# Second attention, last eight steps: score products of two steps in one group, in four banks instead of two

## What is computed

```python
s_sel = jnp.einsum('bgrqd,bgqkd->bgrqk', qb, k_sel) * scale
p_sel = masked_softmax(s_sel, (kpos <= qpos[:, None])[:, :, None])
o_sel = jnp.einsum('bgrqk,bgqkd->bgrqd', p_sel.astype(dt), v_sel)
...
p_win = masked_softmax(s_win, wmask)
o_win = jnp.einsum('bgrqk,bgkd->bgrqd', p_win.astype(dt), v_win)
...
o = g[0] * o_cmp + g[1] * o_sel + g[2] * o_win
```

## Time and profile before

| what | us |
|---|---|
| median of 3 runs (1046.75 to 1049.96) | 1046.78 |
| the profiled execution | 1047.31 |
| its span in the profile | 1045.5 |
| TensorE busy | 1034.8 (99%) |
| VectorE busy | 641.1 (61%) |
| ScalarE busy | 522.2 (50%) |
| GpSimd busy | 346.7 (33%) |

### The profile page before, as it was taken

The page is one execution under the profiler, slowest core; times in us unless marked ns, Lnnn a source line. Parts: engine busy times, 40 slices in busy tenths (PEclk is TensorE's granted clock), DMA queues, the critical chain, the costliest instruction groups (busy, mean ns, idle before and its releaser), DMA issues. The chain is left out here.

```text
span 1045.5 us, 14416 instructions
## 1 busy us (share of the span) xinstructions
PE 1034.8 (99%) x5362; PEld 849.0 (81%) x5362; DVE 641.1 (61%) x1129; ACT 522.2 (50%) x945; POOL 346.7 (33%) x334
## 2 busy tenths in 40 slices
PE   9999999999999999999999999999999999999997
PEld 7788888888878898988787788888888888888885
DVE  5578998666765233514567888344322325999976
ACT  7454345455662333434567874224443446554554
POOL 0022110004330003700264520008779945753542
PEclk9999999999999999999999999999999999999999
DMA  9654322223320384133200461249999942443542
GB/s 331 117 113 118 101 81 71 71 59 124 133 91 1 109 262 141 41 81 81 61 1 2 125 223 55 81 132 326 352 355 339 329 139 61 151 135 137 201 181 82
DMA packets 99639, 146.26 MB, mean 140 GB/s; under 512 B 6209, under 2 KB 60225, under 8 KB 99569
## 3 DMA queue, kind: packets, MB, share of 16 engines
q1 hardware_dynamic: 86016, 129.70, 38.2%
q10 hardware_dynamic: 12768, 12.88, 3.9%
q0 software_dynamic: 784, 2.75, 1.7%
HBM read 123.69 MB, written 21.63 MB: 139 GB/s over the span
## 5 line engine op out<-in xcount | busy, mean ns | idle before, releaser
L2371 DVE TENSOR_TENSOR w_lo<-wring,w_hi 128x1024 fp32r<-128x1024 f32 x32 | 49.0, 1530 | 112.4 <-ACT w_hi L1780 112.4
L1926 DVE TENSOR_TENSOR u_lo<-wring,u_hi 128x1024 fp32r<-128x1024 f32 (+1 forms) x64 | 79.4, 1249 | 53.1 <-ACT u_hi L1505 52.5
L853 PE MATMUL bank<-u_hi,h_hi 128*128 128x512 f32 (+1 forms) x288 | 110.9, 385 | 0.1
L853 PE MATMUL bank<-u_hi,h_lo 128*128 128x512 f32 (+1 forms) x288 | 109.1, 379 | 0.0
L853 PE MATMUL bank<-u_lo,h_hi 128*128 128x512 f32 (+1 forms) x288 | 109.0, 378 | 0.0
L1505 ACT ACTIVATE u_hi<-wring 128x1024 fp32r<-128x1024 f32 (+1 forms) x64 | 65.8, 1032 | 82.7 <-PE bank L853 70.6
L853 PE MATMUL bank<-h_hi,w_lo 128*128 128x512 f32 (+2 forms) x272 | 104.5, 384 | 0.0
L853 PE MATMUL bank<-h_hi,w_hi 128*128 128x512 f32 (+2 forms) x272 | 104.4, 384 | 0.0
L853 PE MATMUL bank<-h_lo,w_hi 128*128 128x512 f32 (+2 forms) x272 | 104.3, 384 | 0.0
L853 PE MATMUL bank<-h_hi,u_hi 128*128 128x512 f32 x224 | 94.1, 420 | 0.3 <-ACT arena L1447 0.2
L1339 PE MATMUL bank<-s_hi,f_hi 128*128 128x512 f32 x224 | 88.5, 395 | 0.1
(11 more groups left out here) (351 smaller groups left out, 2459.4 us busy)
## 6 DMA issues: line engine op xcount, KB each, us to landing
wring<-in_w_in SPq DMA_DIRECT2D x60, 512.0 KB, 3.9
wring<-in_w_ff ACTq DMA_DIRECT2D x12, 1024.0 KB, 8.4
wring<-sums_kept SPq DMA_DIRECT2D x16, 768.0 KB, 4.2
wring<-in_w_ff SPq DMA_DIRECT2D x22, 512.0 KB, 6.1
wring<-in_w_ff SPq DMA_DIRECT2D x32, 256.0 KB, 3.3
sums_kept<-wring SPq DMA_DIRECT2D x22, 256.0 KB, 5.6
arena<-in_w_out SPq DMA_DIRECT2D x4, 1024.0 KB, 5.1
wring<-in_w_out SPq DMA_DIRECT2D x2, 2048.0 KB, 13.0
```

The costliest lines, as they stand in the source:

```text
L853: last = mm(b, lhs, rhs, start=(start and n == 0), stop=(stop and n == 2))
L1926: v.tensor_tensor(u_lo[u % RAW_UNITS][:, 0:cols], raw_unit(u), u_hi[u % HI_UNITS][:, 0:cols].bitcast(F32), ALU.subtract).then_inc(u_lo_don ...
L2371: v.tensor_tensor(cut(w_lo[ring3(m)]), src, cut(w_hi[ring3(m)]).bitcast(F32), ALU.subtract).then_inc(w_lo_done, 1)
```

## The change

In the last eight steps (t from 56, NS - NH), the score products of t = 56 and 58 go out together at t = 56, and those of 60 and 62 at t = 60. The second pair of each group (steps 58, 59, 62, 63) goes to banks 0 and 1, those of the filling products, so TensorE waits for `a_free` at A2_END at t = 56 and t = 60. The waits for `l_done` at t = 58 and 62 fall away. Every pair still raises `s_full` by 2 at its end.

```diff
             i = steps2[u][0]
             at = 256 if i <= 1 and u % 4 >= 2 else 0
-            return bank[2 + u % 2][:, at:at + (i + 1) * P]
+            b = u % 2 if u >= NS - NH and u % 4 >= 2 else 2 + u % 2
+            return bank[b][:, at:at + (i + 1) * P]
...
                 if t < NS:
                     grouped = steps2[t][0] <= 1
-                    if not grouped or t % 4 == 0:
+                    if t % 4 == 0 or not grouped and t < NS - NH:
                         pe.wait_ge(l_done, NS + t)
-                    if not grouped:
+                    if t >= NS - NH and t % 4 == 0:
+                        pe.wait_ge(a_free, A2_END)
+                        pair2(t, 2)
+                        pair2(t + 2, 2)
+                    elif not grouped and t < NS - NH:
                         pair2(t, 2)
                     elif t % 4 == 0:
                         pair2(t, 0)
```

## The result

| | us |
|---|---|
| before, median of 10 (1046.6 to 1049.96) | 1046.96 |
| after, median of 10 (1049.3 to 1052.0) | 1051.01 |
| ratio after to before | 1.0033, 95% interval 1.0024 to 1.0043 |
| profiled execution of after, and its span | 1049.33, 1047.5 |

The kernel became slower: by the ratio 0.33%, 3.5 us (2.5 to 4.5), and by the two medians 4.05 us. The forecast was +2.6. The ten executions of after don't scatter about one value: three lie at 1049.3, the other seven between 1050.5 and 1052.0, and the mean TensorE clock of six of these is 0.997 where that of the three is 0.999. The profiled execution is one of the three, so its trace shows the loss without what the other seven add.

The account below looks back on a forecast made before the run. TensorE, busy 99% of the span, was taken to bound the kernel, with VectorE and ScalarE nearly full in the changed stretch. 2.50 (wait) + 0.13 (legs) = +2.6 us on 1046.78 gave 1049.4 us, range 1047.7 to 1050.9.

Parts of the forecast that it names:

- The new wait: At t = 56 TensorE waits for ScalarE to take the last filling product: pair 56 starts 2.50 us late.
- The lag from the take to TensorE: Before pair 56: TensorE starts 0.65 us after ScalarE's copy of the last filling product starts.
- The legs: Pair 56 to pair 60, 6.37 us against 6.49; pair 60 to branch product, 8.25 against 8.00; together +0.13.
- The order that binds: VectorE's in-order queue sets the first leg, up to pair 60; ScalarE's copies set the second, up to the branch product.
- second leg: From pair 60 to the first branch product: 8.25 us after the change against 8.00 before.
- The change of row mode: Between 64-row and 128-row products, 0.10 us each; falls out inside a group, saving 0.20 us of TensorE's work a group.
- No absorption later: After the branch product: a delay of the attention's last steps reaches the kernel's end in full.
- Rival A: Pair 56 to branch product: TensorE alone binds, late start paid back to +0.9 us, 1047.7; chance 0.15.
- Rival B: Both groups: second pair lies on the chain, nothing given back, +4.1 us, 1050.9; chance 0.15.
- Rival D: At t = 56 the wait costs nothing, only grouping's +0.2 us is left, 1047.0; chance 0.05.
- Rival C: At the stop before pair 56 the clock falls to 1.2 GHz: +2.5, together +5.1 us, 1051.9; chance 0.05.

Follow-up runs that it names:

- the early take: Changed kernel with the last chunk of the last filling product at t = 52 instead of 54, so ScalarE takes it earlier: 1046.88 us, ratio 1.0002.
- e1: The changed kernel again, unaltered, low clock in its trace: five executions from 1050.43 to 1051.19 us, ratio 1.0037 to before.
- e11: The changed kernel once more, unaltered, low clock in its trace: one execution at 1049.36 us, four from 1051.04 to 1051.82, ratio 1.0039 to before.
- the early chunk alone: Kernel before with the last chunk of the last filling product at t = 52 instead of 54, no grouping: 1046.64 us, ratio 0.9999.
- the early-take kernel with the late collect: The early take plus VectorE's collect and GpSimd's addition moved behind scores 58 and 59: 1046.3 us, ratio 0.9993 to before.
- the late collect alone: Kernel before with VectorE's collect and GpSimd's addition moved behind scores 58 and 59, no grouping: ratio 1.0002 to before.

## Why the prediction was right, and where it was not

**The new wait** is what it said, at its place and by its releaser: 2.50 us late forecast, 2.59 measured (pair 52 to pair 56 is 9.56 us against 6.97). The lag from the take to TensorE is 0.74 us (592.06 to 592.80), not 0.65: the one row I took it from the earlier trace rows was 0.1 short for this pair.

**The legs.** Forecast 6.37 and 8.25, measured 6.43 and 8.37: +0.31 against before instead of +0.13. The order that binds is the one named, VectorE's at pair 60 and ScalarE's after; the group at 60 alone shows the second leg's 8.37 again. The change of row mode fell out inside the group, as said.

**No absorption later.** From the branch product to the end of the span: 440.2 us before, 439.9 after. The 2.90 us of the stretch appear in full; that the span grew by only 2.0 is because this run was at pair 52 0.60 us earlier and 0.3 shorter at the end, and traces of other kernels differ by as much.

**Rival A** (TensorE alone binds, +0.9) didn't happen in the changed kernel: it waits 0.51 and 0.45 us again behind the stop. Half of its mechanism is real: with the wait alone, TensorE gains 0.62 us back. **Rival B** (+4.1, both second pairs on the chain) didn't happen either, 14.80 us instead of 16; but 0.93 of its 1.58 us is what grouping costs against the wait alone. **Rival D** is the early take: +0.28 against +0.2 forecast.

**Rival C, the clock, is the step that failed.** I gave it 0.05, and by their times it comes in 16 of 20 executions (two of them traced). The argument was: at the kernel's end the clock fell about four microseconds after the last product, and the stop is 2.5, so it will hold. In the two traces here the clock fell 3.9 us (e1) and 2.3 us (e11) after TensorE had stopped, in e1 when it was at work again. And the one row that the argument rests on is one of a wide spread: in the fourteen traces of this case the clock at the kernel's end falls between 2.2 and 5.2 us after the last product. The shortest is the early chunk alone (last product over at 1038.96), the longest the early-take kernel with the late collect (1038.44). Their windows in which the clock falls, columns as above:

```profile
1041.00:1042.00 1.00, 0.00 (x0) 0.00 (x0) 0.74 (x1) 0.71 (x1) 0.00 (x0) 0.56 0.80 301
```

```profile
1043.00:1044.00 1.00, 0.00 (x0) 0.00 (x0) 0.00 (x0) 0.00 (x0) 0.00 (x0) 0.83 0.53 197
```

Two of the fourteen are shorter than the stop of 2.52 us, so "shorter than four" was no cover. The Trainium skill, page "TensorE: Matmul & The Clock Gate", section "Why this matters for your kernels", warns of stops between bursts, but of longer ones than this; here 2.52 us was enough, and the measurement decides.

C's price was too high for the two traced executions. A low stretch of 3.4 us costs 0.86 and 1.39 us there, not 2.5: it is shorter than the 5 us taken from the kernel's start, and part of it falls on time in which TensorE waits anyway (the wait at pair 60 is 0.27 us in e1 instead of 0.51). The windows at the kernel's start read a granted clock of 1.00, so the earlier trace rows doesn't show what a low clock costs.

**What was luck.** By the ratio the forecast was 0.9 us short, and the time, 1046.78 x 1.0033 = 1050.2, lies in the range. The median of after itself, 1051.01, lies 0.1 above its upper end. That end is rival B's price, and B didn't happen; what brings the time there is C, which the range left out. "Within 0.3%" had 0.73, and 0.33% with an interval from 0.24 to 0.43 doesn't decide it. So the mechanism of the wait and of the legs was right, the traced execution without a low clock (1049.33) is the forecast's 1049.4, and a good part of the upper group's distance from it was not foreseen.

## What to carry to other kernels

A wait that is "already met" where it stands may not be so a few instructions earlier: look up when the releasing engine's queue reaches the release, not when the data were ready. Here the data of (gb, 7) were in PSUM over three microseconds before ScalarE, with exponentials ahead in its queue, took them out. Giving a producer a second pair of banks cost 0.61 us here with the collect ahead in the consumer's queue, and was worth nothing (0.03 us) with it out of the way. And a stop of a few microseconds on TensorE, otherwise 99% busy, must be priced with its clock: behind a stop of 2.52 us it cost another 0.86 and 1.39 us in the two traces, in some executions and not in others. A median then lies in the larger group and hides the other.

## What was not expected of the hardware

After a stop of 2.52 us with TensorE busy on both sides, 14 of 20 executions have a mean clock of 0.997 and 16 are high; in the two of them that were traced the clock is at 0.50 of full speed for 3.4 us, once beginning before work resumed and once 1.4 us after it. None of nine executions with the same stop filled by ten matmuls is high, and none of nine with 1.26 us of stop is at 0.997; one of each was traced. The time from the last product of the kernel to the fall behind it isn't fixed either: 2.2 to 5.2 us in fourteen traces. Single high executions occur in kernels without a stop too (1049.96 and 1049.79 of before, 1049.41 of the late collect alone, 1048.67 of the early take), and two with 0.37 us of stop (1049.36 and 1049.48); none of them was traced.
